# Twenty-seven weight remainders of a split-precision expert projection, moved from GpSimd to VectorE inside a one-hot stage

## The reference

```python
def peer_block(xb, w_q, sub_keys, expert_u, expert_v):
    ...
    eidx = jnp.take_along_axis(cidx, pos, axis=-1)
    gate = jax.nn.softmax(top_s.astype(jnp.float32), axis=-1).astype(xb.dtype)
    u = jnp.take(expert_u, eidx, axis=0)
    act = jax.nn.gelu(jnp.einsum('thkd,td->thk', u, xb))
    v = jnp.take(expert_v, eidx, axis=0)
    return jnp.einsum('thk,thkd->td', gate * act, v)
```

## Time and profile before

| what | value |
|---|---|
| median of three runs | 2866.38 us |
| the three runs | 2866.38, 2867.17, 2862.49 us |
| span of the profiled execution (first to last instruction) | 2861.7 us |
| PE, DVE, ACT, POOL busy over the span | 94%, 78%, 42%, 46% |
| DMA, mean over the span | 173 GB/s |

### The profile page before, as it was taken

One profiled execution on the slowest core, in us unless ns is written; L12 is line 12 of the kernel. 1 busy time (PEld: TensorE's weight loads), 2 busy tenths in 40 slices (PEclk: granted clock), 3 DMA queues, 4 the chain that ended last, 5 costly groups with the idle time before them and its releaser, 6 DMA issues.

```text
span 2861.7 us, 36860 instructions
## 1 busy us (share of the span) xinstructions
PE 2696.6 (94%) x14355; PEld 2238.5 (78%) x14355; DVE 2243.3 (78%) x3548; ACT 1208.4 (42%) x1794; POOL 1326.9 (46%) x859
## 2 busy tenths in 40 slices
PE   8889999999999999999999998999999999999887
PEld 4567777767777788787788988999888888777775
DVE  3688888876878987657569999993777788889875
ACT  3234444443533467733334435664333333333334
POOL 2233333322234544204344766445676776667730
PEclk9999999999999999999999999999999999999998
DMA  7321111134422221023233444777999999999971
GB/s 275 107 70 52 52 52 52 52 118 150 145 74 74 81 67 45 30 89 111 82 102 103 155 156 128 232 245 268 363 372 356 366 359 334 329 329 331 327 262 37
DMA packets 163165, 496.09 MB, mean 173 GB/s; under 512 B 15152, under 2 KB 50992, under 8 KB 162864
## 3 DMA queue, kind: packets, MB, share of 16 engines
q1 hardware_dynamic: 126128, 359.51, 37.4%
q0 software_dynamic: 36864, 134.23, 12.6%
HBM read 443.87 MB, written 49.81 MB: 173 GB/s over the span
## 4 chain that ended last, share of the span: by engine, by line
PE 53%; DVE 27%; DMA 8%; ACT 6%; issue 3%; POOL 3%; SPq 0%; DVEq 0%; ACTq 0%; POOLq 0%
PE ps L800 14%; PE ps L802 14%; PE ps L801 14%; DMA ex<-in_ev,small 4%; DVE oh L2561 3%; DVE ex L1794 2%; DVE ex L2595 2%; PE ps L973 2%; DVE oh L2558 1%; DMA ex<-in_urow,small 1%; DVE oh L2556 1%; DVE pk L2487 1%; PE ps L993 1%; POOL ex L2848 1%; PE ps L947 1%
## 5 line engine op out<-in xcount | busy, mean ns | idle before, releaser
L2682 POOL TENSOR_TENSOR wsp<-ring,wsp 128x1024 fp32r<-128x1024 f32 x219 | 561.1, 2567 | 849.4 <-ACT wsp L1302 823.9
L800 PE MATMUL ps<-hT,wsp 128*128 128x512 f32 (+1 forms) x2040 | 780.8, 383 | 44.2 <-POOL wsp L2682 23.6
L802 PE MATMUL ps<-hT,wsp 128*128 128x512 f32 (+1 forms) x2040 | 752.6, 369 | 0.0
L801 PE MATMUL ps<-hT,wsp 128*128 128x512 f32 (+1 forms) x2040 | 751.7, 368 | 0.0
L800 PEld LDWEIGHTS ps<-hT,wsp 128*128 128x128 f32 x2040 | 387.8, 190 | 117.0 <-issue 32.3
L802 PEld LDWEIGHTS ps<-hT,wsp 128*128 128x128 f32 x2040 | 387.5, 190 | 47.0
L801 PEld LDWEIGHTS ps<-hT,wsp 128*128 128x128 f32 x2040 | 388.5, 190 | 44.2 <-issue 5.0
L1302 ACT ACTIVATE wsp<-ring 128x1024 fp32r<-128x1024 f32 x317 | 331.9, 1055 | 152.0 <-PE ps L802 80.0
L800 PE MATMUL ps<-ex 128*128 128x512 f32 x588 | 233.4, 397 | 29.6 <-DVE ex L1794 26.4
L2848 POOL DMA_INDIRECT ex<-in_ev,small x128 | 194.3, 1518 | 101.1 <-DVE ex L2595 87.6
L2848 POOL DMA_INDIRECT ex<-in_urow,small x128 | 197.8, 1545 | 84.0 <-DVE small L2588 69.4
(11 more groups left out here) (429 smaller groups left out, 5020.5 us busy)
## 6 DMA issues: line engine op xcount, KB each, us to landing
ring<-in_eu SPq DMA_DIRECT2D x128, 512.0 KB
ring<-in_ev SPq DMA_DIRECT2D x128, 512.0 KB
ring<-in_ein SPq DMA_DIRECT2D x57, 512.0 KB
gd<-oh SPq DMA_DIRECT2D x6, 4096.0 KB, 14.2
ex<-gd SPq DMA_DIRECT2D x32, 768.0 KB
ring<-in_oin SPq DMA_DIRECT2D x39, 512.0 KB
ring<-in_ada SPq DMA_DIRECT2D x30, 512.0 KB
ex<-zd SPq DMA_DIRECT2D x20, 768.0 KB, 9.6
```

The source lines that it names most:

```text
L800: pe.matmul(out, W[0], R[0], start=first, stop=False)
L801: pe.matmul(out, W[0], R[1], start=False, stop=False)
L802: return pe.matmul(out, W[1], R[0], start=False, stop=last)
L2682: pool.tensor_tensor(s[:, 1, :], raw_of(i), s[:, 0, :].bitcast(F32), ALU.subtract).then_inc(pool_done, G.step("lo", i))
```

## The change

```diff
         def by_pool(name, u):
 
             return (name in ("ein", "wq") or name == "eout" and u % 2 == 0 or name in ("win", "wo") or name == "oin" and not 16 <= u < 22 or name == "oin" and u == 18
-                    or name == "eu" and u < NPRE * JC)
+                    or name == "eu" and u < NPRE * JC and not SOFT + 3 <= u < SOFT + 30)
```

## The result

The changed kernel takes 3000.1 us (median of 4 runs, 2991.91 to 3008.02), the kernel before 2866.78 us (4 runs). The ratio is 1.0467, 95% interval 1.0444 to 1.049: 133 us slower, where 15 us faster was forecast, with a range up to 2860.

What follows compares the result with a forecast made beforehand. DVE was taken to bound the one-hot stage, 31% of its time waiting for POOL. Gains of 2.8 us (stage start) and 12.3 (tile intervals) sum to 15.1: 2866.4 becomes 2851.3 us, own range 2848 to 2855, whole range up to 2860.

Steps and rivals of the forecast that it cites:

- Queued behind the new waits: On DVE in the one-hot stage: low parts ahead of each tile's five operations wait for nothing, except at tiles 7 and 15.
- the two places above: Ahead of tiles 7 and 15, DVE's second low part waits for ACT's hi; PE waits 1.7 us each, 3.4 us together.
- The stretch is POOL's, 2.20 us each: DVE's one-hot operations take 3.41 us instead of 1.21 when POOL's low part holds the shared port; 28 stretches, 61.5 us.
- The rival of "slower": DVE's long one-hot operations come from something other than POOL, so DVE gets 30.8 us more: 2897 us; chance 0.03.
- DVE's tile 5.80 + 1.14 = 6.94, PE's 7.00: One-hot stage: five operations plus one low part on DVE stay just under PE's tile, so PE becomes the bound.
- Intervals 173.5 us of PE's own, 176.9 with the two waits: PE's 23 intervals from tile 0 to tile 23 shrink from 189.2 us to 176.9: 12.3 us gained.
- Start of the stage, 2.8 us gained: PE starts tile 0 at 1755.0 instead of 1757.8, as POOL's four low parts no longer lie in it.
- Loads late behind the stores: Rival: closer stores make the load behind each of six land 1 us late, 6 us lost: 2857 us; chance 0.07.
- The clock: One PE gap with its clock fallen (0.57 of full speed, 1848 to 1852) goes away, already counted in the 189.2 us.
- The first: Rival, DVE stays the bound: 0.3 us more semaphore exchange with ACT per low part costs 7 us: 2858; chance 0.12.
- if DVE waits for ACT's hi in most tiles: One sign, to be seen in the one-hot stage, that would show the prediction wrong; no size given.

Runs made afterwards that it cites:

- no low parts: The kernel before without the low parts of blocks 43 to 69 on either POOL or DVE (output not the reference's): 2847.01 us, ratio 0.9933.
- e1_late: The changed kernel with DVE's low parts one unit later, lo(u + 1) instead of lo(u + 2) ahead of the tile: 2850.7 us, ratio 0.9945.
- e2_pairs: As e1_late, but at tiles 7 and 15 the second low part is made behind the tile: 2848.93 us, ratio 0.995.
- e8_both: The changed kernel with DVE's low parts one unit later and ACT's hi(u + 3) made right behind the gelu of u: 2848.68 us, ratio 0.9938.
- e5_warm: The changed kernel with 19 extra matmuls on PE ahead of each hot tile, their sums overwritten: 2982.1 us, ratio 1.0391.
- e3_wait: The kernel before, all low parts on POOL, with DVE only waiting for hi(u + 2) behind the piece pre of u: 3041.55 us.

## Why the prediction was wrong

**The step that failed** is under *Queued behind the new waits*: "In the steady state it waits for an hi that ended about 1.3 us before DVE is free (5.67 against 7.00), so nothing, except at the two places above." It rests on the place of the low parts in DVE's list, taken from the piece pre alone. With the default behind each piece, DVE stands one unit ahead, and the wait that the prediction worked out for tiles 7 and 15 (DVE ready 12.7 us after the tile before, with the hi done at 5.67) holds at every tile. The turn of 12.69 us at full clock is that same sum. The mechanism had been seen and priced; it was put at two places, and it holds in 22 of the 23 intervals.

Point by point:
- *The stretch is POOL's, 2.20 us each:* right (no low parts: all gone). The rival of "slower" that denied it was the wrong one to guard against.
- *DVE's tile 5.80 + 1.14 = 6.94, PE's 7.00:* right, 6.94 in e1_late.
- *Intervals 173.5 us of PE's own, 176.9 with the two waits:* right for the order meant, 173.3 (e2_pairs) and 176.4 (e1_late); each of the two waits lengthens its interval by 1.5 us and not 1.7. In the changed kernel the same intervals take 321.7 us.
- *Start of the stage, 2.8 us gained:* wrong for the changed kernel. lo(45) waits for an hi behind one more gelu. From the start of DVE's last operation ahead of the stage to tile 0 on PE took 16.5 us before and takes 19.4. For the order meant the term was too large: 15.2 us in e1_late, 1.3 us gained. There hi(44) came 7.0 us after that operation and not 5.5 as before; why it did stays open.
- *Loads late behind the stores:* did not happen; ACT did not wait for a load at the stage's hi in the changed kernel, nor in e1_late, where the tiles came as close as forecast. In e8_both it did, five times and for up to 1.9 us, and PE did not wait for it.
- *The clock:* taken as a gain (one slow gap less). With a turn of 13.6 us PE idles 5 us in each, and the low clock came in 23 of the 24 tiles.
- *The rivals:* none put a wait at the head of DVE's queue at every tile. The first named the exchange with ACT, but priced it by the length of a semaphore's exchange and not by what ACT has in front of the hi. The list of what would prove the text wrong did hold "if DVE waits for ACT's hi in most tiles".

POOL's rows of before do not show the place. POOL has nothing else to do in this stage, so its low parts start when their hi is done wherever they stand in its list (118.5 us idle, all ended by ACT's hi); the code shows how far ahead it runs. An engine that is idle hides the order of its queue, and that order becomes a cost when the work moves to one that is busy. The hi at 1786.39, behind the copies, gave the price; what was missing was a look at what calls the piece.

**What beats both kernels:** the change together with the later place, 2850.7 (e1_late), 2848.93 (e2_pairs) or 2848.68 (e8_both), some 0.5 to 0.6% below before. Between the three the times decide nothing.

## What to carry to other kernels

Moving an operation to another engine moves its wait too: write down what stands behind it in the new queue, and follow the chain from there until it ends or comes back to itself. If it comes back, the length of the turn is the time of a step, however little each engine has to do, and placing the operation one step later can open it. Read every function that runs at that place, the default as well as the piece, before counting how far ahead an engine is.

## What the runs showed of the hardware

In the changed kernel PE waited 23 times for 4.4 to 5.1 us, and each time the 48 matmuls behind the wait took 4.3 to 5.2 us, where they take 2.93 us at full clock. Before, PE waited six times for 2.3 to 3.1 us, and only one wait was followed by the low clock, and not the longest:

```profile
1847.62 4.50 PE L1208 MATMUL ps<-oh 128*128 128x128 bf16 x48 [2.60 <-DVE oh L2561]
```

With matmuls in the gap (e5_warm) the granted clock was 1.00 from tile 0 to tile 23. The low clock cost 0.95 us a tile, and it made the circle longer, since the late matmuls delay the copies that delay the hi.

The Trainium skill says of VectorE and GpSimd (SBUF — State Buffer, section "SBUF: two separate sides") that whichever starts first holds the shared ports for its whole instruction. The rows of e3_wait agree: DVE started 0.05 us ahead of POOL, ran its 1.23 us unhindered, and POOL took 3.40 us where it needs 2.40 alone; then DVE's next operation took 3.38. The prediction also weighed what the Trainium skill says in Perfetto Trace Analysis, section "Optimizing Scalar/DVE Operations": take work off a saturated VectorE, but between VectorE and GpSimd, which share a port, this might not help. The runs side with the second half: with the circle open, the work that came from POOL to a DVE at 99% made the kernel faster by some 16 us (e1_late, ratio 0.9945).
